# Opening of a two-layer decoder trunk on one core: first loads on two queues, tile 0 scaled in one go, fewer angle instructions

## The reference

```python
def rms_norm(x, g):
    y = x * lax.rsqrt(jnp.mean(x * x, axis=-1, keepdims=True) + EPS)
    return y * g

# hybrid_mixer, layer l:  u = rms_norm(h, mix_norm_pre[l]) @ w_in[l]
#   attention heads, a convolution module and dilated attention follow, side by side
def rope(x, positions):
    inv_freq = ROPE_THETA ** (-jnp.arange(half) / half)
    ang = positions[..., None] * inv_freq
    cos, sin = jnp.cos(ang), jnp.sin(ang)
    ...
# then: cross-attention into 256 memory tokens, and a gated feed-forward layer with a convolution
```

## Time and profile before

| | |
|---|---|
| median of 3 runs | 834.75 us (834.73 to 834.96) |
| profiled execution: own time | 834.92 us |
| profiled execution: span of the trace | 832.5 us |
| PE / PEld / DVE / ACT / POOL busy | 824.6 / 735.5 / 616.0 / 496.9 / 28.8 us |
| chain that ended last | PE 97%, issue 1%, ACT 1%, DVE 1% |
| DMA | 147.33 MB, mean 177 GB/s |

### The profile page before, as it was taken

The page is one execution under the profiler, slowest core; times in us unless marked ns, Lnnn a source line. Parts: engine busy times, 40 slices in busy tenths (PEclk is TensorE's granted clock), DMA queues, the critical chain, the costliest instruction groups (busy, mean ns, idle before and its releaser), DMA issues.

```text
span 832.5 us, 13059 instructions
## 1 busy us (share of the span) xinstructions
PE 824.6 (99%) x5181; PEld 735.5 (88%) x5181; DVE 616.0 (74%) x1077; ACT 496.9 (60%) x765; POOL 28.8 (3%) x52
## 2 busy tenths in 40 slices
PE   9999999999999999999999999999999999999997
PEld 6998988888889999988899889888988899999885
DVE  6799986755676888777386999848568488877653
ACT  5646875656555665655365588655656466666441
POOL 1200000100010000000020000001000000000000
PEclk9999999999999999999999999999999999999999
DMA  8854345472473565556657453446545536555661
GB/s 320 318 188 152 102 132 171 145 279 66 151 245 128 178 199 181 202 173 208 201 176 247 154 152 118 141 148 222 182 126 176 180 107 202 198 191 171 204 192 51
DMA packets 40780, 147.33 MB, mean 177 GB/s; under 512 B 4688, under 2 KB 4816, under 8 KB 40720
## 3 DMA queue, kind: packets, MB, share of 16 engines
q1 hardware_dynamic: 38592, 138.91, 51.6%
q0 software_dynamic: 2128, 7.59, 2.7%
HBM read 145.43 MB, written 1.05 MB: 176 GB/s over the span
## 4 chain that ended last, share of the span: by engine, by line
PE 97%; issue 1%; ACT 1%; DVE 1%; DVEq 0%; POOLq 0%; POOL 0%; ACTq 0%
PE acc L1488 7%; PE acc L1489 7%; PE acc L1490 7%; PE acc L1471 5%; PE acc L1473 5%; PE acc L1472 5%; PE acc L1528 4%; PE acc L1530 4%; PE acc L1529 3%; PE psAB L1471 3%; PE psAB L1472 3%; PE psAB L1473 3%; PE psCD L1424 3%; PE psAB L1490 3%; PE psAB L1489 3%; PE psAB L1488 3%
## 5 line engine op out<-in xcount | busy, mean ns | idle before, releaser
L882 DVE TENSOR_TENSOR wlo<-raw,whi 128x1024 fp32r<-128x1024 f32 x240 | 289.5, 1221 | 90.8 <-ACT whi L498 89.1
L498 ACT ACTIVATE whi<-raw 128x1024 fp32r<-128x1024 f32 x240 | 249.7, 1056 | 112.5 <-PE acc L1473 45.8
L1488 PE MATMUL acc<-xT_hi,whi 128*128 128x256 f32 x432 | 123.4, 286 | 0.0
L1489 PE MATMUL acc<-xT_lo,whi 128*128 128x256 f32 x432 | 122.2, 283 | 0.0
L1490 PE MATMUL acc<-xT_hi,wlo 128*128 128x256 f32 x432 | 122.2, 283 | 0.0
L1488 PEld LDWEIGHTS acc<-xT_hi,whi 128*128 128x128 f32 x432 | 82.8, 192 | 2.9 <-issue 2.3
L1489 PEld LDWEIGHTS acc<-xT_lo,whi 128*128 128x128 f32 x432 | 82.8, 192 | 0.1
L1490 PEld LDWEIGHTS acc<-xT_hi,wlo 128*128 128x128 f32 x432 | 82.8, 192 | 0.0
L1488 PE MATMUL psCD<-xT_hi,whi 128*128 128x256 f32 x192 | 54.6, 285 | 0.0
L1490 PE MATMUL psCD<-xT_hi,wlo 128*128 128x256 f32 x192 | 54.3, 283 | 0.0
L1489 PE MATMUL psCD<-xT_lo,whi 128*128 128x256 f32 x192 | 54.3, 283 | 0.0
(11 more groups left out here) (288 smaller groups left out, 2017.8 us busy)
## 6 DMA issues: line engine op xcount, KB each, us to landing
raw<-stream_dram SPq DMA_DIRECT2D x256, 512.0 KB, 4.1
gpre<-gain_dram POOLq DMA_DIRECT2D x7, 512.0 KB, 5.9
gpost<-gain_dram POOLq DMA_DIRECT2D x6, 512.0 KB, 5.2
h<-x_dram SPq DMA_DIRECT2D x2, 512.0 KB, 5.7
memn<-mem_dram SPq DMA_DIRECT2D x2, 512.0 KB, 10.1
out_dram<-h SPq DMA_DIRECT2D x4, 256.0 KB, 2.0
cst<-const_dram SPq DMA_DIRECT2D x1, 896.0 KB, 5.4
gpre<-gain_dram SPq DMA_DIRECT2D x1, 512.0 KB, 5.9
```

The source lines that it names most:

```text
L498: act.activation(home(g)[0], raw[:, s * GW:(s + 1) * GW], ACT.Copy).then_inc(w_hi.sem, 1)
L882: dve.tensor_tensor(lo, raw[:, cols], hi.bitcast(F32), ALU.subtract).then_inc(w_lo.sem, 1)
L1488: pe.matmul(dst, whi[:, cols], hi[:, toks], start=k == 0 and c % 2 == 0, stop=False)
L1489: pe.matmul(dst, whi[:, cols], lo[:, toks], start=False, stop=False)
```

## The change

SyncE issues x's tile 0 first, then the gain's row, then group 0. Position and constants are issued by ScalarE, ahead of everything else it does. On ScalarE the sine moves ahead of the split of group 0, and both copies of tile 0's flips stand together behind that split and ahead of the split of group 1. On VectorE both halves of tile 0 are scaled one behind the other, then group 0 is split, both low inputs are made, group 1 is split. The angles take two instructions where there were four, twice, and one where there were two, with operands of three dimensions. TensorE makes 19 idle products, the first flip, 1 idle product, the second flip, and then passes: three each for groups 0 and 1 of tile 0, two each for groups 2 and 3, `low_w` of group 2, flips of tile 1, the four high passes of tile 1, `low_w` of group 3 of tile 0, and the eight low passes of tile 1 as before.

```diff
--- before.py
+++ after.py
@@ -394,11 +394,9 @@
             def x_rows(t):
                 sp_.dma_start(h[:, t * D:(t + 1) * D], x[t * P:(t + 1) * P, :]).then_inc(x_in[t].sem, 16)
 
-            sp_.dma_start(posi[:, :], pos).then_inc(pos_in.sem, 16)
-            sp_.dma_start(cst[:, 0:CC_TRI], consts[:, 0:CC_TRI]).then_inc(head_in.sem, 16)
             x_rows(0)
+            sp_.dma_start(gpre[:, :], gains[0, MIX_PRE, :].partition_broadcast(P)).then_inc(gain0_in.sem, 16)
             group(0)
-            sp_.dma_start(gpre[:, :], gains[0, MIX_PRE, :].partition_broadcast(P)).then_inc(gain0_in.sem, 16)
             group(1)
             x_rows(1)
             group(2)
@@ -519,16 +517,18 @@
                 act.wait_ge(xt_tr.sem, 2 * t + b + 1)
                 act.activation(chunks(xT_hi, b, t), blocks(psCD[b]), ACT.Copy).then_inc(xt_hi.sem, 1)
 
+            act.dma_start(posi[:, :], pos).then_inc(pos_in.sem, 16)
+            act.dma_start(cst[:, 0:CC_TRI], consts[:, 0:CC_TRI]).then_inc(head_in.sem, 16)
             act.wait_ge(half_set.sem, 1)
             own.link(act.activation(junk[:, 0:1], st(S_POW), ACT.Sin))
             squares_x(0)
-            split_group(0, 0)
             act.wait_ge(trig_arg.sem, 1)
             act.activation(trig[:, :], trig[:, :], ACT.Sin).then_inc(trig_ready.sem, 1)
-            first_input_hi(0, 0)
+            split_group(0, 0)
+            for b in range(2):
+                first_input_hi(0, b)
             split_group(0, 1)
             squares_x(1)
-            first_input_hi(0, 1)
             split_group(0, 2)
             split_group(0, 3)
             for b in range(2):
@@ -891,16 +891,15 @@
             dve.wait_ge(head_in.sem, 16)
             dve.wait_ge(pos_in.sem, 16)
             own.link(dve.tensor_copy(posf, posi[:, :]))
+            by_kind = lambda a: a.rearrange("p (t k n) -> p k t n", t=TOK, k=2)
             for t in range(TOK):
-                for k in range(2):
-                    e = dve.tensor_scalar(ang[:, (2 * t + k) * HALF:(2 * t + k + 1) * HALF],
-                                          cst[:, CC_FRQ:CC_FRQ + HALF], posf[:, t:t + 1], None, ALU.mult)
+                e = dve.tensor_scalar(ang[:, 2 * t * HALF:2 * (t + 1) * HALF].rearrange("p (k n) -> p k n", k=2),
+                                      cst[:, CC_FRQ:CC_FRQ + HALF].unsqueeze(1).to_broadcast([P, 2, HALF]),
+                                      posf[:, t:t + 1], None, ALU.mult)
             own.link(e)
-            for t in range(TOK):
-                for k in range(2):
-                    cols = slice((2 * t + k) * HALF, (2 * t + k + 1) * HALF)
-                    e = dve.tensor_scalar(turns_[:, cols], ang[:, cols], float(1 / (2 * np.pi)), 0.25 if k == 0 else 0.0,
-                                          ALU.mult, ALU.add)
+            for k in range(2):
+                e = dve.tensor_scalar(by_kind(turns_)[:, k], by_kind(ang)[:, k], float(1 / (2 * np.pi)),
+                                      0.25 if k == 0 else 0.0, ALU.mult, ALU.add)
             own.link(e)
             nearest = 1.5 * 2.0 ** 23
             own.link(dve.tensor_scalar(turns_, turns_, nearest, -nearest, ALU.add, ALU.add))
@@ -910,10 +909,7 @@
             part3 = float(2 * np.pi - part1 - part2)
             for c in (part1, part2, part3):
                 own.link(dve.scalar_tensor_tensor(ang, turns_, -c, ang, ALU.mult, ALU.add))
-            for t in range(TOK):
-                cols = slice(2 * t * HALF, (2 * t + 1) * HALF)
-                e = dve.tensor_scalar(ang[:, cols], ang[:, cols], float(np.pi / 2), None, ALU.add)
-            own.link(e)
+            own.link(dve.tensor_scalar(by_kind(ang)[:, 0], by_kind(ang)[:, 0], float(np.pi / 2), None, ALU.add))
             pi = 3.1415925
             dve.tensor_scalar(trig[:, :], ang, pi, -pi, ALU.min, ALU.max).then_inc(trig_arg.sem, 1)
 
@@ -964,13 +960,13 @@
                                   ALU.subtract).then_inc(xt_lo.sem, 1)
 
             norm_input(0, 0, 0)
-            first_scale(0, 0)
+            for n in range(2):
+                first_scale(0, n)
             split_group(0, 0)
-            first_input_lo(0, 0)
-            first_scale(0, 1)
+            for b in range(2):
+                first_input_lo(0, b)
             split_group(0, 1)
             norm_input(0, 0, 1)
-            first_input_lo(0, 1)
             split_group(0, 2)
             for n in range(2):
                 first_scale(1, n)
@@ -1448,10 +1444,11 @@
                 for i in range(n):
                     pe.matmul(accs[1][0][:, :], idle[:, 0:P], idle[:, :], start=True, stop=True)
 
-            idle_products(24)
+            idle_products(19)
             pe.wait_ge(head_in.sem, 16)
             first_input(0)
-            idle_products(5)
+            idle_products(1)
+            first_input(1)
 
             for l in range(DEPTH):
                 def product(g0, groups, lhs, outs, k0=0, k_of=KC, width=NT, order=None):
@@ -1641,21 +1638,18 @@
                         return e
 
                     both_hi, low_x, low_w = (True, True), (True, False), (False, True)
-                    first_pass(both_hi, 0, 0)
-                    first_pass(low_x, 0, 0)
-                    first_pass(low_w, 0, 0)
-                    first_input(1)
-                    for g in range(1, PER_TILE):
+                    for g in range(2):
                         first_pass(both_hi, g, 0)
                         first_pass(low_x, g, 0)
-                        if g < PER_TILE - 1:
-                            first_pass(low_w, g, 0)
+                        first_pass(low_w, g, 0)
+                    for g in range(2, PER_TILE):
+                        first_pass(both_hi, g, 0)
+                        first_pass(low_x, g, 0)
+                    first_pass(low_w, 2, 0)
                     inputs(0, 1)
-                    first_pass(both_hi, 0, 1)
-                    first_pass(both_hi, 1, 1)
-                    first_pass(low_w, PER_TILE - 1, 0)
-                    first_pass(both_hi, 2, 1)
-                    first_pass(both_hi, 3, 1)
+                    for g in range(PER_TILE):
+                        first_pass(both_hi, g, 1)
+                    first_pass(low_w, 3, 0)
                     for g in range(PER_TILE):
                         first_pass(low_x, g, 1)
                         first_pass(low_w, g, 1).then_inc(w_used.sem, 1)
```

## The result

The changed kernel takes 836.77 us (median of 14 runs, 835.91 to 837.82), the kernel before 834.74 in the same job (14 runs, 834.32 to 835.01): a ratio of 1.0026, 95% interval 1.0018 to 1.0034. It is slower by 2.0 us, not faster by 1.75. The profiled execution took 837.37, with a span of 834.9.

A forecast was written before the change was run, and what follows sets the result against it. TensorE, busy 824.6 of 832.5 us, bounds the kernel: its opening plus fixed work. Order (1.25) and queues (0.5) start tile 1's flips 1.75 us earlier, taking the median from 834.75 to 833.0; 8-in-10 range 832.65 to 833.9.

The forecast's parts named there:

- the first loads: Start of the opening: x's tile 0 issued first lands at 4.65 to 5.3, taken as 5.05; the queues give 0.5 us.
- Two of its own signs of being wrong: Opening: the prediction is wrong if, among others, the angles end behind 6.6 us or passes go at 0.9 us.
- rival B: Opening loads: group 0 or constants late, beyond 0.4 or 0.6 us of slack; 833.35 to 834.05; chance 0.12.
- Rival C: TensorE's opening passes: waiting drops the clock from 2.4 to 1.2 GHz, a pass costs 0.91 us; 836.85; chance 0.05.
- F: The moment TensorE starts the flips of tile 1: 17.80 us before the change, forecast 16.05.
- The order of scaling, flips and passes: Opening: the new order alone, x landing at 5.55 still, gives 1.25 us of the 1.75.
- ScalarE's chain sets F: Opening: ScalarE's copies, splits and squares run without waiting from 9.92 us, ready at 14.65; three passes later F is 16.05.
- Group 0: Opening: this weight group lands at 8.0 us, between 7.6 and 8.4; ScalarE must start its split by 8.48.
- The angle instructions: VectorE's opening: fewer instructions take 2.55 us rather than 3.15, worth nothing unless the constants land behind 3.99.
- Two issues on ScalarE ahead of its table load: ScalarE's opening: some 0.9 us more, ready at 3.15 instead of 2.24, before x lands; cost nothing.
- The shift goes through whole: Behind the opening: TensorE's later waits are fractions of a microsecond, so the 1.75 us gain reaches the end.
- The idle products' end: TensorE's opening: 19 idle products instead of 24 end five pitches earlier, so the first flip can start at 8.55 us.

## Why the prediction was wrong

*Step that failed: the first loads.* The prediction saw that constants and x would be in flight together and asked only what this costs x. It bounded x's landing from both sides, 4.65 to 5.3, and took 5.05; measured 5.04 (0.74 + 4.3). For the constants it took 3.4, the landing of before, when nothing else was in flight, and gave no bounds for the operation that was new: a load of small rows on a second queue beside one of large rows. It landed at 7.14. It reckoned the disturbance in bytes and engine time (80 KB, some 0.6 us), where turns of packets decide: 256 small rows, each behind a large one. Two of its own signs of being wrong came: the angles ended at 9.84, behind 6.6, and three passes took 0.85 to 0.99.

*What came after was priced rightly, and not used.* The prediction gives 3.99 as the landing from which the constants push the norm, and rival B says of it "from there each costs one to one". With 7.14 it gives 3.15 us on top of 833.0, 836.15. But B got a chance of 0.12, and its price ended at 834.05, where the loads' landings had been left within a microsecond of before. Measured against the kernel with the angles out of the way, the norm was 3.30 late (9.76 against 6.46) and the second flip 3.28 (12.52 against 9.24).

*The clock.* Rival C, the lower clock, got 0.05 and its own cause, the wait of 0.7 behind the first pass. That wait came (0.63 idle ahead of the pass at 11.28 in the kernel with late angles) and did nothing: the passes behind it went at 0.46. That C's price, 836.85, lies 0.08 from the measured median is luck. What brought the clock down was a wait of 3.33 behind the idle products, a consequence of B. The two rivals weren't independent, and their sum was the likeliest way to be slower: 836.15 and 0.64 to 0.86 are 836.8 to 837.0, measured 836.77. The lower clock cost far less than in rival C, which had put F 3.85 behind the forecast (19.9 against 16.05), since it lasted for 3.4 us only and not for eleven passes, and ScalarE's chain had slack in front of F, as the prediction had said. Of the Trainium skill's rule (TensorE: Matmul & The Clock Gate, Part 1: The HAM clock gate) the trace now shows both halves, the fall behind 3.3 us without work too; waits of up to 1.68 in the kernels above left the clock alone.

*Right, with their sizes:*

- The order of scaling, flips and passes: 1.25 was forecast with x landing as before; 1.0 measured with the constants back in front (833.76), x having landed 0.25 later there.
- ScalarE's chain sets F: with late angles the flips started at 16.07, forecast 16.05, and 6.20 behind the copy of the second flip (9.87), forecast 6.13 (the terms in the prediction add up to 6.10, so its F should read 16.02). The sum of the gain, 1.75, was measured as soon as the constants were in nobody's way (1.65 to 2.0 in three kernels, 1.46 where the late sine took some of it back).
- Group 0: taken up at 8.20 to 8.32 in the three profiles with the new queues in which ScalarE waited for it, forecast 8.1 with 8.48 as the bound. With position first on SP it came once at 8.75, behind that.
- The angle instructions: 2.68 instead of 3.15 us, forecast 2.55. Worth nothing in the kernel with the constants in front, where VectorE idled for 1.18 us between them and the norm; in the changed kernel, bound by the constants, they gave 0.47 back.
- Two issues on ScalarE ahead of its table load: ready at 3.15 (2.95 + 0.21), forecast 3.15, under cover.
- The shift goes through whole: F +2.36, product +2.35, span +2.4.
- The idle products' end, 8.55 forecast, is not a fixed time: see below.

## What to carry to other kernels

A load of few bytes on a second queue isn't small if it has many rows: beside a queue full of 4 KB packets each of its packets waits a turn, so 1 KB in 128 rows cost nearly as much as 80 KB in 128 rows, some 2 us each, and the work behind both moved from 3.4 to 7.1 us. Issue such loads ahead of the large ones, or move what needs them out of the critical engine's program. Here either was enough (833.05 and 832.85, not told apart by their intervals); the second was open because the engine that was on the path (VectorE) held work that nobody needed before the rotary step, long after the opening, in front of work that everybody waited for. When a change puts something in flight beside something else, bound the landing of both, and when one rival is a late input, add to it what the idle engine will cost afterwards.

## What the runs showed of the hardware that wasn't expected

- Two hardware queues take turns by packets: 145 and 149 packets of the second beside 173 and 177 of the first between 2.0 and 4.5 us, with 0.01 and 0.08 MB in them.
- TensorE's granted clock fell to a mean of 0.67 over 5.1 us after 3.33 us without work, to 0.50 over 5.6 us after 3.81, and fell after 4.08 with the two loads swapped; waits of 1.48 and 1.68 (with x held back) left the passes at 0.46. The moment of the fall differs: 1.7 us into the new work in the first, at about 11.2 us, still within the wait, in the other two. The lower level lasted for 3.4, 6.8 and 3.4 us.
- The time until TensorE's products come at the fast pace at the start of a kernel varies, though the granted clock is written as 1.00 throughout: the same 19 idle products, begun at 1.46, took 7.03 in the changed kernel, 6.33 with late angles, 6.01 with the two loads swapped, 7.45 in the kernel with one queue. Filling a wait with a fixed number of products sets no fixed time, and where they last longest they delay the first flip (8.74 there, with its data ready before 8.1).
- x's tile 0, issued first, landed after 3.9 us with one queue (one profile) and after 4.1 to 4.4 beside the small loads of the second (six profiles). How much of that is the second queue's is open, since x, third in one queue, took 3.9 in the kernel before and 4.2 with the constants back on SP.
